# First norm's weights issued by ScalarE, second weight unit split by two engines, gates' columns in parts

## The chip, the cores and the metric

The kernel runs on one core of a Trainium2 chip. The metric is the time of one execution on the device in microseconds (us), the median of several runs. One launch computes the whole reference.

## The reference, cut to what matters

Two blocks work on 256 tokens of width 1024. The first has two layers, each a norm, a mixer (a chunkwise mLSTM with a causal convolution beside a sliding window attention) and an MLP. The second block has two more kinds of attention and a layer that gathers experts. The change touches the head of both layers of the first block:

```python
h = rmsnorm(x, norm_mix_g[l])                  # the first norm's weights are norm_mix_g[0]
proj = h @ w_in[l]
mqk, mv, mo, mi, mf, aq, ak, av, ga, gb = jnp.split(proj, offsets, axis=-1)
...
ig = mi + b_igate ; logf = log_sigmoid(mf + b_fgate)     # the gates, 4 heads
b = jnp.cumsum(fc, axis=-1)
dmat = jnp.where(tril, b[..., :, None] - b[..., None, :] + ic[..., None, :], -jnp.inf)
m_comb = jnp.maximum(m_inter, jnp.max(dmat, axis=-1))
w_intra = jnp.exp(dmat - m_comb[..., None])
s = jnp.einsum('bhld,bhsd->bhls', qc, kc) * w_intra
```

## The kernel before, in words

**Weights come in units.** A unit is 128 x 2048 numbers (1 MB). `layer_units` gives their order in a layer: two of the values (mv 0, mv 1), four mqk, mv 2 and mv 3, four queries (aq 0 to 3), the keys ak, the values av, then the rest. SyncE (SP) issues one DMA per unit into one of three raw slots (`unit_dma`, L470); a slot is free when the signal lo_ready has counted its last user. ScalarE (ACT) rounds the unit to w_hi (`split_hi`, L546), VectorE (DVE) makes the rest w_lo = raw - w_hi (`split_lo`, L553), and TensorE (PE) multiplies in three passes (`passes`, L579 to L581). In some places Pool makes the rest instead (`split_lo_by_pool`, L575). All engines run their own program in order and meet by semaphores; there is no planner.

**The start of layer 0.** SP issues the first tile of tokens x (L479), the first norm's weights, one row of 4 KB given to 128 partitions (L483), the first unit in two halves (L507), the second tile of tokens, and then the units. ACT issues the DMA of the small parameters (L1534, `columns`), squares tile 0 (L684, `norm_act`), rounds both halves of unit 0 (L560, `first_hi`), rounds the transposed tokens (L715, `tile_act`), squares tile 1 and rounds unit 1 (`split_hi`). DVE norms tile 0 (L700, `norm_dve`), makes the rests of unit 0 (L566, `first_lo`) and of the tokens (L721, `tile_dve`), then the rest of unit 1, and only then norms tile 1. Pool makes constants, waits for the small parameters to turn one part of them round (L1524), and then makes one over the root of each tile's mean square (L690 and L693, `norm_pool`). PE transposes tile 0 (L708), multiplies tile 0 with units 0 and 1, in the middle of that transposes tile 1, and multiplies tile 1 with both (`by_tile`). Every engine's order is the order of its program.

**The gates, in both layers.** After mqk 3 PE makes the gates' product. ACT and DVE turn it into rows of 4 x 256; the last one on DVE is L1200 (signal gate_m). Behind unit aq 0 PE spreads each head's row over 128 partitions (`gate_columns`, L834): four products of depth 4, which the profile shows as eight instructions, into the banks att 0 and att 1. In the middle of unit aq 1 it turns the other rows into columns (`gate_more_columns`, L841; signal columns_done). Behind aq 1 stand two products of keys and queries (`kq`, L853 and L854), whose first waits for acol_ready: the copy by DVE of these columns to memory (L1218, in `decay`).

The order of ACT around it is: round a later unit, take aq 0 out of its bank when that unit is done (`take`, L1053), four sigmoids of the convolution (L992, behind a table load), round the next unit but one (L546), take aq 1. DVE's order is: the rest of that unit (L553), then `decay`. Pool multiplies the sigmoids into qk (L1481, eight times 128 x 256) from the first sigmoid on.

Of the kernel before, what the change touches and what calls it, by code (L numbers as in the profile page):

```python
# [7 lines left out]
F32 = mybir.dt.float32  # L8
# [3 lines left out]
ALU = mybir.AluOpType  # L12
# [3 lines left out]
P = 128  # L16
D, SEQ, DEPTH = 1024, 256, 2
# [24 lines left out]
UNIT = 2048  # L42
# [19 lines left out]
def ring_places():  # L62
# [17 lines left out]

    "hi_ready": "a unit's rounded part is made", "lo_ready": "and the rest of it: its raw slot is free",
    "first_hi": "the rounded part of half of the first unit", "first_lo": "and the rest of it",
    "first_loaded": "half of the first unit is here", "x_loaded_too": "the second tile of tokens is here",
    "unit_done": "TensorE is through with a unit", "tile_done": "and with its first tile of tokens", "emptied_act": "ScalarE has emptied a product's bank",
    "emptied_dve": "VectorE has emptied a product's bank",
# [178 lines left out]
class Counts:  # L264
# [10 lines left out]
    def mark(self, name, key=0, by=1):  # L275

        assert (name, self.scope, key) not in self.where, (name, key)
        self.total[name] = self.total.get(name, 0) + by
        self.where[name, self.scope, key] = self.total[name]
        return by  # L280
# [17 lines left out]
def build(nc, A, out, known):  # L298
# [5 lines left out]
    with ctx:  # L304
# [158 lines left out]
        def unit_dma(sp, u):  # L463

            g = counts.unit(u)
            src = A["units2"][u * P:(u + 1) * P, :] if counts.scope == "second" else A["units"][counts.scope, u * P:(u + 1) * P, :]
            if LAST_AT_HOME[g] is not None:
                sp.wait_ge(S["lo_ready"], LAST_AT_HOME[g] + 1)
            s = HOME[g]
            sp.dma_start(raw[s], src).then_inc(S[f"w_loaded{s}"], mark(f"w_loaded{s}", u, 16))  # L470

        def sync_program(sp):
            def rows_of(w):
                return w.broadcast_to([P, D])
# [5 lines left out]
                        S["x_loaded" if t == 0 else "x_loaded_too"], 16)  # L480

            tokens(0)
            sp.dma_start(g_next, rows_of(A["norm_mix_g"][0:1, :])).then_inc(S["g_loaded"], mark("g_loaded", "mix", 16))  # L483
            for l in range(DEPTH):
                counts.scope = l
                for u, unit in enumerate(units):
# [69 lines left out]
        def first_hi(act, half):  # L556

            cols = slice(half * UNIT // 2, (half + 1) * UNIT // 2)
            act.wait_ge(S["first_loaded" if half == 0 else f"w_loaded{HOME[0]}"], 16)
            nc.scalar.copy(w_hi[:, SLOT[0], cols], raw[HOME[0]][:, cols]).then_inc(S["first_hi" if half == 0 else "hi_ready"], 1)  # L560

        def first_lo(dve, half):

# [232 lines left out]
        def layer_pe(pe, l):  # L796
            def step(u, first_time=True):

                name, i, kind = units[u]
                if first_time:  # L800
                    if (l, u) == (0, 0):
                        pe.wait_ge(S["first_lo"], 1)
                    else:
                        pe.wait_ge(S["lo_ready"], counts.unit(u) + 1)
                    for p in BEFORE.get((name, i), []):
                        emptied(pe, *p)
                    if name == "wo" and i < 2:
                        pe.wait_ge(S["y_lo"], at("y_lo", 2 * i + 1))
                    if name == "down" and i % 2 == 0:
                        pe.wait_ge(S["ff_lo"], at("ff_lo", i + 1))  # L810
                xh, xl = (xb_hi, xb_lo) if name in ("bm", "wo", "down") else (xa_hi, xa_lo)
                return BANKS[name, i], SLOT[counts.unit(u)], xh, xl
# [15 lines left out]
                               k == 0, k == KT - 1)  # L828
                m.then_inc(S["gate_done"], mark("gate_done"))

            def gate_columns():
                pe.wait_ge(S["gate_m"], at("gate_m"))
                for h in range(M_HEADS):
                    nc.tensor.matmul(att[h // 2][:, (h % 2) * SEQ:(h % 2 + 1) * SEQ], ident[0:M_HEADS, h:h + 1].broadcast_to([M_HEADS, P]), g_M,  # L834
                                     start=True, stop=True)

# [81 lines left out]
            for u, (name, i, kind) in enumerate(units):  # L918
                if (name, i) in (("mv", 1), ("wo", 3), ("up", 1), ("down", 15)):
                    continue  # L920
                if (name, i) == ("mv", 0):
                    by_tile(pe, step, u, (0, 4), (True, False), (False, True), "mv",
                            lambda t: tile_pe(pe, "mix", 1) if t == 0 else None, "mix", l == 0)
                elif (name, i) == ("wo", 2):
                    by_tile(pe, step, u, (0, 4), (True, False), (False, True), "wo", lambda t: tile_pe(pe, "mlp", 0) if t == 1 else None)
                elif (name, i) == ("up", 0):
                    by_tile(pe, step, u, (0, 4), (True, False), (False, True), "up", lambda t: tile_pe(pe, "mlp", 1) if t == 0 else None, "mlp")
                elif (name, i) == ("down", 14):
                    by_tile(pe, step, u, (4, 4), (False, False), (True, True), "down",
                            lambda t: early_tile(l + 1) if t == 1 and l + 1 < DEPTH else None)  # L930
                else:
                    b, s, xh, xl = step(u)
                    j = TURNED_WITHIN.get((name, i))
                    within = {("gb", 3): turn_hm, ("aq", 1): gate_more_columns}.get((name, i), lambda: None)
                    between = within if j is None else (lambda: turn_probs(j))
                    if name in ("ga", "gb") or name == "up" and i >= 4:
                        unit_wide(b, s, xa, ("u", u), between)
                    elif kind == "F":
                        unit_f(b, s, xh, xl, ("u", u), {("bm", 0): "hm", ("ba", 0): "ha"}.get((name, i)), between)
                    elif kind == "V":  # L940
                        unit_v(b, s, xh, xl, ("u", u))
                    elif name == "down":
                        unit_t(b, s, xh, xl, 4 * (i // 2 % 2), i < 2, False, ("u", u))
                    else:
                        unit_t(b, s, xh, xl, 4 * (i % 2), i % 2 == 0, i % 2 == 1, ("u", u), between)
                if (name, i) in TURNED_WITHIN:
                    pv(TURNED_WITHIN[name, i])
                if (name, i) in SCORED_AFTER:
                    scores(SCORED_AFTER[name, i])
                if (name, i) == ("mqk", 3):  # L950
                    gate_products()
                elif (name, i) == ("aq", 0):
                    gate_columns()
                elif (name, i) == ("aq", 1):
                    kq(0)
                    kq(1)
                elif (name, i) == ("aq", 3):
                    num_product(0)
                    kq(2)
                elif (name, i) == ("ak", 0):  # L960
                    num_product(1)
                    kq(3)
                elif (name, i) == ("av", 0):
                    num_product(2)
                elif (name, i) == ("mo", 0):
                    num_product(3)
                elif (name, i) == ("up", 2):
                    turn_up()


        def layer_act(act, l):
# [111 lines left out]
            if l == 0:  # L1083
                norm_act(act, "mix", 0)
                first_hi(act, 0)
                first_hi(act, 1)
                tile_act(act, xa_hi, "mix", 0)
                norm_act(act, "mix", 1)
                split_hi(act, 1)
            else:  # L1090
                split_hi(act, 0)
                norm_act(act, "mix", 0)
                split_hi(act, 1)
                tile_act(act, xa_hi, "mix", 0)
                norm_act(act, "mix", 1)
                split_hi(act, 2)
# [68 lines left out]
        def layer_dve(dve, l):  # L1165
# [222 lines left out]
                    S["emptied_dve"], mark("emptied_dve", ("wo", 2 * half + t)))  # L1388

            if l == 0:  # L1390
                dve.wait_ge(S["g_loaded"], at("g_loaded", "mix", "start"))
                norm_dve(dve, "mix", 0, g_next)
                for half in range(2):
                    first_lo(dve, half)
                    tile_dve(dve, xa_hi, xa_lo, "mix", 0, [half])
                split_lo(dve, 1)
                norm_dve(dve, "mix", 1, g_next)
            else:
                split_lo(dve, 0)
                mlp_add(dve, l - 1, 0, 0)  # L1400
# [69 lines left out]
        def layer_pool(pool, l):  # L1470
            norm_pool(pool, "mix", 0)
            if l > 0:
                split_lo_by_pool(pool, 1)
            norm_pool(pool, "mix", 1)

            nc.gpsimd.memset(mv[:, :, :, M_DV:VW], 1.0).then_inc(S["pads_ready"], mark("pads_ready", 0))
            nc.gpsimd.memset(mqk[:, :, 0:CONV_K - 1], 0.0).then_inc(S["pads_ready"], mark("pads_ready", 1))
# [53 lines left out]

        def start_act(act):
            counts.scope = "start"
            act.dma_start(columns[:], A["columns"]).then_inc(S["params_loaded"], mark("params_loaded", 0, 16))  # L1534

        def start_dve(dve):
# [864 lines left out]
```

## Time and profile before

| what | value |
|---|---|
| median of 3 runs | 1753.12 us (1752.78 to 1753.4) |
| profiled execution, its own time | 1752.94 us |
| its span, first to last instruction | 1751.2 us |
| mean granted clock of TensorE | 0.985 of full speed |
| busy: PE, PE weight loads, DVE, ACT, Pool | 92%, 68%, 66%, 48%, 22% |
| DMA, mean over the span | 265 GB/s; some 420 GB/s in the last third |

Times in rows are microseconds from the start of the span. A bracket behind a row gives the engine's idle time before it and what ended it. The clock of a stretch is given as a share of 2.4 GHz. In the first two thirds of the span PE is busy nearly throughout and the DMA engines are not; in the last third, where experts are gathered, it is the other way round.

### The profile page before, as it was taken

Reading aid. Unit: us, or ns where it says so; the run is one execution under the profiler, and the core shown is the slowest. Engines: PE = TensorE matmul, PEld = TensorE weight load, DVE = VectorE, ACT = ScalarE, POOL = GpSimd, SP = SyncE. Lnnn points to the kernel's source line nnn. Section 1 sums busy time; section 2 is a strip of 40 time slices with the busy share of each in tenths; the row PEclk is TensorE's granted clock in tenths of the full one; section 3 lists DMA queues with packets and bytes.
Section 4 is the critical chain, followed back from the end, with each engine's and each line's share of the span. In section 5 each row is a group of like instructions: output and inputs, shape, how many; then the busy total and the mean of one; then the engine's idle time right before and its main releaser. Section 6 shows DMA issues by size and latency. Waiting matters only on the chain.

```text
span 1751.2 us, 21314 instructions
## 1 busy us (share of the span) xinstructions
PE 1613.2 (92%) x8160; PEld 1183.5 (68%) x8160; DVE 1159.2 (66%) x2030; ACT 835.1 (48%) x1555; POOL 379.0 (22%) x374
## 2 busy tenths in 40 slices
PE   7999999999999999999999999799987788778786
PEld 6998998888898899888889998455522232222232
DVE  5757865666665776566675556788676767767654
ACT  4456635333455664533355545454444444444443
POOL 0100001000120000100050102565543444334440
PEclk9999999999999999999999999999999999999999
DMA  7444454555544355455544365999999999999996
GB/s 293 161 144 145 152 209 155 198 185 187 198 166 140 125 183 214 168 193 192 186 151 145 145 217 194 414 421 421 422 421 421 422 421 422 422 421 422 421 421 270
DMA packets 67206, 464.43 MB, mean 265 GB/s; under 512 B 7457, under 2 KB 9633, under 8 KB 11809
## 3 DMA queue, kind: packets, MB, share of 16 engines
q0 software_dynamic: 36864, 268.45, 36.9%
q1 hardware_dynamic: 29952, 194.29, 30.8%
q8 instruction: 64, 1.05, 0.2%
q10 hardware_dynamic: 288, 0.33, 0.1%
q14 instruction: 38, 0.30, 0.0%
HBM read 462.00 MB, written 1.05 MB: 264 GB/s over the span
## 4 chain that ended last, share of the span: by engine, by line
PE 65%; DMA 21%; DVE 6%; issue 4%; ACT 3%; POOL 0%; SPq 0%; POOLq 0%; ACTq 0%
PE acc L579 13%; PE acc L581 13%; PE acc L580 13%; DMA arena<-in_peer_uv,arena 10%; DMA row_w_lo<-in_peer_uv,arena 5%; PE att L604 5%; DMA row_w_hi<-in_peer_uv,arena 4%; PE acc L1718 4%; PE acc L1721 4%; PE acc L604 3%; PE att L605 3%; PE acc L605 1%; DVE w_lo L553 1%; DVE arena L2132 1%; PE att L904 1%
## 5 line engine op out<-in xcount | busy, mean ns | idle before, releaser
L553 DVE TENSOR_TENSOR w_lo<-arena,w_hi 128x2048 fp32r<-128x2048 f32 x171 | 391.7, 2300 | 172.8 <-ACT w_hi L546 172.5
L546 ACT CAST w_hi<-arena 128x2048 fp32r<-128x2048 f32 x175 | 333.6, 1907 | 121.8 <-PE acc L581 100.2
L1840 ACT ACTIVATE arena<-arena 128x1 f32<-128x1 f32 x256 | 51.9, 203 | 322.7 <-DVE arena L2132 139.5
L2132 DVE SCALAR_TENSOR_TENSOR arena<-arena 128x1024 f32<-128x1024 f32 x114 | 139.3, 1223 | 84.9 <-DMA arena<-in_peer_uv,arena 83.1
L579 PE MATMUL acc<-xa,w_hi 128*128 128x256 f32 x672 | 192.9, 287 | 0.0
L580 PE MATMUL acc<-xa,w_lo 128*128 128x256 f32 x672 | 190.8, 284 | 0.0
L581 PE MATMUL acc<-xa,w_hi 128*128 128x256 f32 x672 | 190.7, 284 | 0.0
L1718 PE MATMUL acc<-arena,gate_raw 128*128 128x512 f32 x226 | 128.1, 650 | 46.8 <-ACT gate_raw L1850 46.3
L2326 POOL DMA_INDIRECT arena<-in_peer_uv,arena x114 | 129.6, 1137 | 151.4 <-PE acc L1721 141.1
L604 PE MATMUL att<-xa,w_hi 128*128 128x512 f32 x384 | 136.0, 398 | 0.0
L579 PEld LDWEIGHTS acc<-xa,w_hi 128*128 128x128 f32 x672 | 129.2, 192 | 3.6 <-issue 3.0
L580 PEld LDWEIGHTS acc<-xa,w_lo 128*128 128x128 f32 x672 | 129.2, 192 | 0.2
L581 PEld LDWEIGHTS acc<-xa,w_hi 128*128 128x128 f32 x672 | 129.2, 192 | 0.0
L579 PE MATMUL acc<-w_hi,xb 128*128 128x512 f32 x320 | 125.2, 391 | 0.0
L581 PE MATMUL acc<-w_lo,xb 128*128 128x512 f32 x320 | 124.7, 390 | 0.0
L580 PE MATMUL acc<-w_hi,xb 128*128 128x512 f32 x320 | 124.6, 389 | 0.0
L1721 PE MATMUL acc<-arena,gate_raw 128*128 128x512 f32 x226 | 120.8, 617 | 0.0
L579 PE MATMUL acc<-xb,w_hi 128*128 128x256 f32 (+1 forms) x336 | 114.1, 340 | 0.4 <-DVE xb L721 0.4
L1850 ACT ACTIVATE gate_raw<-ident,arena 128x128 f32<-128x128 f32 x255 | 102.4, 401 | 23.4
L1718 PEld LDWEIGHTS acc<-arena,gate_raw 128*128 128x128 f32 x226 | 37.5, 197 | 112.1 <-ACT gate_raw L1850 96.3
L690 POOL TENSOR_TENSOR small<-small 128x1 f32<-128x1 f32 x11 | 2.7, 245 | 494.9 <-ACT arena L684 494.9
L605 PE MATMUL att<-xa,w_lo 128*128 128x256 f32 x384 | 107.8, 281 | 0.0
(309 smaller groups left out, 3545.7 us busy)
## 6 DMA issues: line engine op xcount, KB each, us to landing
arena<-in_units SPq DMA_DIRECT2D x175, 1024.0 KB, 4.8
arena<-in_bias SPq DMA_DIRECT2D x1, 2048.0 KB, 9.3
arena<-in_peer_uv,arena POOLq DMA_INDIRECT x114
x_res<-in_x SPq DMA_DIRECT2D x2, 512.0 KB, 6.5
arena<-in_norm_mix_g SPq DMA_DIRECT2D x2, 512.0 KB, 6.9
arena<-in_units SPq DMA_DIRECT2D x2, 512.0 KB, 8.1
arena<-in_norm_mlp_g SPq DMA_DIRECT2D x2, 512.0 KB, 6.6
arena<-in_norm_g SPq DMA_DIRECT2D x2, 512.0 KB, 5.8
```

Of the source, the lines that this page charges most:

```text
L546: nc.scalar.copy(w_hi[:, s, :], raw[HOME[g]]).then_inc(S["hi_ready"], 1)
L553: nc.vector.tensor_tensor(w_lo[:, s, :], raw[HOME[g]], w_hi[:, s, :].bitcast(F32), ALU.subtract).then_inc(S["lo_ready"], 1)
L579: nc.tensor.matmul(out_, lh, rh, start=first, stop=False)
L580: nc.tensor.matmul(out_, ll, rh, start=False, stop=False)
L581: return nc.tensor.matmul(out_, lh, rl, start=False, stop=last)
L604: nc.tensor.matmul(banks[n_], h[:, k, col_], x2[:, :, k, :], start=k == 0, stop=False)
L605: m = nc.tensor.matmul(banks[n_][:, 0:SEQ], lw[:, k, col_], x2[:, 0, k, :], start=False, stop=k == 7)
L1718: m = nc.tensor.matmul(row_sums[t][0][:], diag[n % 4], rows_ring[PLACE[n]][:, D:D + 512], start=first, stop=last)
L1721: nc.tensor.matmul(row_sums[t][1][:], diag[n % 4], rows_ring[PLACE[n]][:, D + 512:ROW], start=first, stop=last).then_inc(S["rows_multiplie ...
L1850: nc.scalar.activation(diag[n % 4], ident[:], ACT.Copy, scale=d).then_inc(S["diag_ready"], 1)
L2132: nc.vector.scalar_tensor_tensor(row, row, 1.0, hn[:, n // SLOTS, :], ALU.mult, ALU.mult, accum_out=dots[:, n:n + 1]).then_inc(S["rows_use ...
L2326: nc.gpsimd.indirect_dma_start(rows_ring[PLACE[n]], None, A["peer_uv"], bass.IndirectOffsetOnAxis(ap=expert[:, n:n + 1], axis=0)).then_inc ...
```

## The change

Three edits. The DMA of the first norm's weights goes from SP's queue to ACT's, as the first thing that ACT does, under a signal of its own. In layer 0 the second unit is rounded by ACT in two halves, DVE makes the rest of the first half and Pool that of the second, and DVE norms tile 1 ahead of that instead of behind. In both layers two of the four heads' gate rows are spread in the middle of unit aq 0, and the other two behind it.

```diff
@@ sync_program
             tokens(0)
-            sp.dma_start(g_next, rows_of(A["norm_mix_g"][0:1, :])).then_inc(S["g_loaded"], mark("g_loaded", "mix", 16))
@@ unit_dma
+            if LAST_AT_HOME[g] == 1:
+                sp.wait_ge(S["first_lo"], 2)
@@ new functions
+        def second_hi(act, half):
+            cols = slice(half * UNIT // 2, (half + 1) * UNIT // 2)
+            if half == 0:
+                act.wait_ge(S[f"w_loaded{HOME[1]}"], at(f"w_loaded{HOME[1]}", 1))
+            nc.scalar.copy(w_hi[:, SLOT[1], cols], raw[HOME[1]][:, cols]).then_inc(S["first_hi" if half == 0 else "hi_ready"], 1)
+
+        def second_lo(eng, op, half):
+            cols = slice(half * UNIT // 2, (half + 1) * UNIT // 2)
+            if half == 0:
+                eng.wait_ge(S["first_hi"], 2)
+            else:
+                eng.wait_ge(S["hi_ready"], 2)
+                eng.wait_ge(S["lo_ready"], 1)
+            op(w_lo[:, SLOT[1], cols], raw[HOME[1]][:, cols], w_hi[:, SLOT[1], cols].bitcast(F32), ALU.subtract).then_inc(
+                S["first_lo" if half == 0 else "lo_ready"], 1)
@@ layer_pe, step
                         pe.wait_ge(S["first_lo"], 1)
+                    elif (l, u) == (0, 1):
+                        pe.wait_ge(S["first_lo"], 2)
+                        pe.wait_ge(S["lo_ready"], 2)
@@ layer_pe, gate_columns
-            def gate_columns():
+            def gate_columns(heads):
                 pe.wait_ge(S["gate_m"], at("gate_m"))
-                for h in range(M_HEADS):
+                for h in heads:
@@ layer_pe, units
-                    within = {("gb", 3): turn_hm, ("aq", 1): gate_more_columns}.get((name, i), lambda: None)
+                    within = {("gb", 3): turn_hm, ("aq", 0): lambda: gate_columns((0, 1)), ("aq", 1): gate_more_columns}.get((name, i), lambda: None)
...
                 elif (name, i) == ("aq", 0):
-                    gate_columns()
+                    gate_columns((2, 3))
@@ layer_act, l == 0
                 norm_act(act, "mix", 1)
-                split_hi(act, 1)
+                second_hi(act, 0)
+                second_hi(act, 1)
@@ layer_dve, l == 0
-                dve.wait_ge(S["g_loaded"], at("g_loaded", "mix", "start"))
+                dve.wait_ge(S["g_first_loaded"], 16)
...
-                split_lo(dve, 1)
                 norm_dve(dve, "mix", 1, g_next)
+                second_lo(dve, nc.vector.tensor_tensor, 0)
@@ layer_pool
             norm_pool(pool, "mix", 1)
+            if l == 0:
+                second_lo(pool, nc.gpsimd.tensor_tensor, 1)
@@ start_act
+            act.dma_start(g_next, A["norm_mix_g"][0:1, :].broadcast_to([P, D])).then_inc(S["g_first_loaded"], 16)
             act.dma_start(columns[:], A["columns"]).then_inc(S["params_loaded"], mark("params_loaded", 0, 16))
```

## Rows read from the trace of the kernel before

**Rows 1.** The page, part 1: busy time, share of the span, instructions of each engine.
```profile
PE 1613.2 (92%) x8160; PEld 1183.5 (68%) x8160; DVE 1159.2 (66%) x2030; ACT 835.1 (48%) x1555; POOL 379.0 (22%) x374
```

**Rows 2.** The chain that ended last, first 20 us: start us, us, what.
```profile
3.27 11.14 DMA arena<-in_units
14.43 1.91 ACT w_hi L546
16.36 2.30 DVE w_lo L553
```

**Rows 3.** Timeline of the first 8 us: SP's and ACT's issues, Pool, DVE.
```profile
0.80 0.40 ACTq L1534 DMA_DIRECT2D columns<-in_columns  x1
1.23 0.42 SPq L483 DMA_DIRECT2D arena<-in_norm_mix_g  x1
...
4.83 0.31 POOL L1524 TENSOR_SCALAR columns<-columns 128x32 f32<-128x32 f32 x1 [3.04 <-DMA columns<-in_columns]
...
7.46 1.41 DVE L700 SCALAR_TENSOR_TENSOR arena<-x_res,small,arena 128x512 f32<-128x512 f32 x2 [7.46 <-DMA arena<-in_norm_mix_g]
```

**Rows 4.** Windows: stretch, us, busy of the engines, clock, DMA share, GB/s.
```profile
5.00:6.00 1.00, 0.00 (x0) 0.00 (x0) 0.00 (x0) 0.71 (x2) 0.32 (x2) 1.00 0.91 229
...
13.00:14.00 1.00, 0.93 (x2) 0.83 (x3) 1.00 (x2) 0.74 (x2) 0.18 (x1) 1.00 1.03 434
```

**Rows 5.** Timeline of 10 to 21 us: all engines around unit 1.
```profile
10.67 1.04 ACT L560 CAST w_hi<-arena 128x1024 fp32r<-128x1024 f32 x1 [0.20 <-DMA arena<-in_units]
...
14.19 0.56 POOL L693 TENSOR_TENSOR small<-small,minus_half 128x1 f32<-128x1 f32 x1
...
17.91 0.63 PE L581 MATMUL acc<-w_lo,xa 128*128 128x512 f32 x1
18.57 1.41 DVE L700 SCALAR_TENSOR_TENSOR arena<-x_res,small,arena 128x512 f32<-128x512 f32 x2
...
18.71 0.49 PE L579 MATMUL acc<-w_hi,xa 128*128 128x512 f32 x1 [0.17 <-DVE w_lo L553]
...
20.89 1.03 PE L708 MATMUL att<-ident,arena 128*128 128x128 f32 x8
```

**Rows 6.** Pool by source line: ns min/median/max; L575 all, L1481 at 73 to 77 and 77 to 80.2.
```profile
L575 POOL TENSOR_TENSOR w_lo<-arena,w_hi x4: 4595/4596/5057, 267.8 to 1076.5; 128x2048 fp32r<-128x2048 f32 x4
...
L1481 POOL TENSOR_TENSOR arena<-arena x5: 632/727/737, 73.8 to 76.4; 128x256 f32<-128x256 f32 x5
...
L1481 POOL TENSOR_TENSOR arena<-arena x3: 732/737/2684, 76.4 to 77.8; 128x256 f32<-128x256 f32 x3
```

**Rows 7.** Timeline of PE at aq 0 and aq 1, both layers, and one window of layer 0.
```profile
71.10 1.99 PE L834 MATMUL att<-arena,ident 4*128 4x256 f32 x8
73.02 0.41 PE L579 MATMUL acc<-xa,w_hi 128*128 128x256 f32 x1
...
77.59 1.05 PE L841 MATMUL att<-ident,arena 4*128 4x4 f32 x8
...
508.18 0.39 PE L579 MATMUL acc<-xa,w_hi 128*128 128x256 f32 x1
...
511.25 1.05 PE L841 MATMUL att<-ident,arena 4*128 4x4 f32 x8
...
74.00:75.00 1.00, 1.00 (x7) 1.00 (x6) 0.00 (x0) 1.00 (x3) 1.00 (x2) 0.50 0.83 319
```

**Rows 8.** Timeline: gate_m on DVE, then aq 0 taken and the first kq, both layers.
```profile
66.70 0.41 DVE L1200 SCALAR_TENSOR_TENSOR arena<-arena 4x256 f32<-4x256 f32 x1
...
71.21 0.60 ACT L1053 ACTIVATE arena<-acc 128x512 f32<-128x512 f32 x1 [1.15 <-PE acc L581]
...
81.53 0.59 PE L853 MATMUL att<-arena 128*128 128x256 f32 x2
...
506.37 0.60 ACT L1053 ACTIVATE arena<-acc 128x512 f32<-128x512 f32 x1 [1.15 <-PE acc L581]
...
515.40 0.30 PEld L853 LDWEIGHTS att<-arena 128*128 128x128 f32 x2 [0.24 <-DVE small L1218]
```

More of the change, by code:

```diff
@@ L82 @@
     "first_hi": "the rounded part of half of the first unit", "first_lo": "and the rest of it",
+    "g_first_loaded": "the first norm's weights are here",
     "first_loaded": "half of the first unit is here", "x_loaded_too": "the second tile of tokens is here",
```

## The prediction

> **What bounds the kernel now.** I read the page first: PE is busy 92% of the span and no other engine comes near it [rows 1]. So an edit counts where PE is late or waits, and in the first two layers a microsecond that PE loses or gains is handed on to the end: ACT, DVE and the weight DMAs there wait for PE's signals. The three edits lie at two kinds of place, and I read each from the view that shows who comes last there.
>
> At the start I took the chain of waits. Its first 20 us are the DMA of unit 1, landed at 14.43, ACT's rounding, DVE's rest, and then PE at 18.71 [rows 2, 5]. PE comes off unit 0 just before: its last product of that starts at 17.91, and it then shows 0.17 us of idle [rows 5]. The start is balanced: PE is not waiting long, and whoever makes unit 1 ready later than 18.7 makes the kernel longer.
>
> At the gates I took the timeline of PE. The eight small products hold PE from 71.10 to 73.02, and behind them PE's granted clock is 0.50, that is 1.2 GHz instead of 2.4, though PE had no gap ahead of that [rows 7]. The cost can be read by laying the layers side by side, as layer 1 keeps its clock: from the first product of aq 1 to the block in its middle it is 77.59 - 73.02 = 4.57 us in layer 0 and 511.25 - 508.18 = 3.07 in layer 1, so the low clock costs 1.50 us [rows 7].
>
> What comes behind that matters as much. The first kq waits for DVE's copy of the columns. In layer 1 PE's weight load stands idle 0.24 us for it [rows 8]: there the side chain, aq 0 taken by ACT, sigmoids, rounding, DVE's rest, copy, already comes last. It runs from 506.37 to 515.40, 9.03 us [rows 8]. In layer 0 the same distance is 81.53 - 71.21 = 10.32 us with no wait of PE, as PE is the slow one there [rows 8].
>
> **Edit 1, the DMA on ACT's queue.** SP loses one issue of 0.42 us [rows 3], and x's second tile, units 0 and 1 are issued that much earlier. The bytes stay the same and the 16 DMA engines are at a share of 0.91 and 1.03 in the stretches around the transfers [rows 4], so they gain from 0 to 0.45 us. I take 0.2: unit 1 lands at 14.2, since the engines are nearer to full than to empty. ACT issues one DMA more (0.40 us, [rows 3]), while it has nothing but its table load to do before the tokens arrive: nothing. The small parameters are now queued behind the 512 KB of norm weights. Pool waits for them at 4.83 ahead of the root that tile 0's norm needs, and the norm weights landed at 7.46 [rows 3]; if both land at 7.5, Pool is through (0.31 and under 1 us, [rows 3, 5]) at 8.8, and DVE's norm starts 1.3 us later than 7.46. What hides it is ACT, which takes the transposed tile only behind its second half of unit 0, whose rounding ends at 11.7 [rows 5]. I count nothing; beyond some 1.5 us of delay it would show one for one. If the tokens land later, since they now share the engines with the norm weights, the same cover holds.
>
> **Edit 2, unit 1 in halves.** Before, PE starts on it 18.71 - 14.43 = 4.28 us behind the landing [rows 2, 5]. Now ACT rounds two halves of 1.04 us [rows 5], so both are there 2.1 us behind the landing, at 16.3. Pool takes 4.596 us for a whole unit [rows 6], 2.3 for half: twice DVE's 2.30 per unit [rows 2]. Alone, Pool is done at 16.3 + 2.3 = 18.6, PE starts at 18.7, and the split has bought nothing. DVE's norm of tile 1 starts when the root is there, 14.19 + 0.56 = 14.75 [rows 5], ends at 16.2, and DVE's half (1.2 us) follows until 17.4.
>
> The unknown is how Pool and DVE get on. At 77 to 80 us, while DVE makes a rest, one of Pool's products of 0.73 takes 2.68 us, with the shape of five others at 0.63 to 0.74 [rows 6]. The extra 1.95 us is nearly a whole rest of DVE (2.30, [rows 2]), so I read it as one waiting for the other. DVE's half starts at 16.2 and Pool's wants to at 16.3, so one goes after the other: 16.2 + 1.2 + 2.3 = 19.7, or 19.5 when unit 0 and with it the square of tile 1 come 0.2 earlier. PE starts unit 1 at 19.5 in place of 18.7: **+0.8 us**. The bounds are -0.4 (no hindrance, DMA gain in full) and +1.0. The other order, Pool first, gives the same sum. The Trainium skill, SBUF — State Buffer, section "SBUF: two separate sides", says that a VectorE instruction with two SBUF inputs and a GpSimd instruction that reads SBUF take the shared port pair as "an exclusive lock, not a bandwidth split". By that rule it is the sum above; were it a split in which each slows by a quarter, it would be 19.2, and +0.5.
>
> The norm of tile 1, moved ahead, was not late: it ran at 18.57 for 1.41 us, to 19.98, and PE came to the transposes at 20.89 [rows 5]. Nothing gained. SP's wait for unit 4's slot has a condition more, and it is met before Pool's half is: nothing.
>
> **Edit 3, the rows in two places.** gate_m is made by 66.70 + 0.41 = 67.1 [rows 8], and the middle of aq 0 is some 3 us ahead of 71.0, at 68.1: PE doesn't wait, with 1 us to spare. The weak stretch is cut in half, to 0.96 us, as long as the other block, L841 with 1.05, behind which the clock stood [rows 7]. So the clock stays up in layer 0, and PE reaches kq 1.50 earlier, at 80.0.
>
> But aq 0 is now done half a block later: 0.96 us, with the way in and out 1.1. ACT's take, the sigmoids, the rounding, DVE's rest and the copy all stand behind that. Layer 0: 71.21 + 1.1 + 9.03 = 81.3; PE waits there 1.3 us and starts at 81.3 in place of 81.53: **-0.2**. Layer 1 had no low clock to win back and was already waiting: **+1.1**, bounds +0.9 and +1.2.
>
> **Sum:** 0.8 - 0.2 + 1.1 = +1.7 us. On the profiled execution 1752.94 gives 1754.6; its own time is 0.18 below the median, and against the median 1753.12 I get 1754.8. Its own range is 1753.8 to 1755.4. About 0.2%, 3.5 us, is what a measurement of this kernel can tell from no change, so this is within it.
>
> **Rivals.** (a) Slower: the waits that the change makes (some 1.4 us ahead of unit 1, 1.3 ahead of kq in either layer) let the clock down or keep it down. Each time costs 1.50 [rows 7]: 1756.3 for one, 1757.8 for two. It decides from the point where a wait is followed by products at 0.50. For it: the clock did fall behind weak work; against: each wait has full work before and behind it. The Trainium skill, TensorE: Matmul & The Clock Gate, part 1 on the clock gate, has the low clock as the default that activity releases and idleness brings back; by that the fall at 73, without idleness, is not explained, and the new waits are the danger.
> (b) Pool and DVE don't hinder each other: the start costs 0 to -0.4 in place of +0.8, and the sum is +0.5 to +0.9, 1753.8. Against it is the product of 2.68 us.
> (c) Faster: the side chain isn't what holds kq, the 1.50 comes in full, layer 1 stays, the start gives 0.4: 1751.2. Against it is the wait of 0.24 us.
> (d) The third edit doesn't do what it says: the clock falls in layer 0 all the same. PE is then at kq at 81.6, and the sum is +2.0: 1755.1.
>
> **Numbers.** The forecast has a chance of 0.50, (a) 0.17, (b) 0.15, (c) 0.07, (d) 0.08; 0.03 is for the unforeseen. The range runs from 1752.9, under (b), to 1756.7, over (a) with one fall. Over 1756.6 needs two falls or more: 0.07. Faster by over 0.2% would be under 1749.6, which no case reaches: 0.02. The rest, 0.91, is no change.
>
> **What would show it.** Right: Pool's half starts when DVE's ends, PE's first product of unit 1 at 19.2 to 19.8; no window of 0.50 behind 71; PE idle ahead of kq 1.0 to 1.5 us in both layers, released by DVE L1218; aq 0 taken 1.1 us later against gate_m in both. Wrong: Pool and DVE side by side with the durations of [rows 6]; PE on unit 1 before 18.5; a kq without a wait; a window of half clock in layer 0 or 1 outside the first 19 us.

## The result, and the profile after

The changed kernel takes 1758.19 us (median of 9 runs, 1756.3 to 1758.76), the kernel before 1752.78 in its 9 runs of the same series (1751.36 to 1754.05). The ratio is 1.0027, with a 95% interval from 1.0017 to 1.0037: slower, by 5.4 us in the medians and by 4.7 by the ratio, where 1.7 were forecast and 1756.7 us was the upper end of the range. The profiled execution took 1758.48 us, its span 1756.7.

The page after, part 1, against [rows 1]: the work is the same, and what grew is the time in which PE does nothing.

```profile
span 1756.7 us, 21318 instructions
...
PE 1611.7 (92%) x8160; PEld 1181.7 (67%) x8160; DVE 1160.2 (66%) x2030; ACT 835.2 (48%) x1556; POOL 381.3 (22%) x375
```

I put the k-th product of PE after beside the k-th before. PE starts tile 1 on unit 0 at 26.51 us, where it was 22.89: 3.6 us are lost in the first 27. At the gates of layer 1 the shift rises from 3.7 to 4.97 us, it is 5.18 at 993 us, and it ends at 5.5.

**The start after**, timeline of the first 21 us, against [rows 3] and [rows 5]:

```profile
0.80 0.41 ACTq L1560 DMA_DIRECT2D arena<-in_norm_mix_g  x1
1.24 0.45 ACTq L1561 DMA_DIRECT2D columns<-in_columns  x1
...
6.40 1.06 ACT L704 ACTIVATE arena<-x_res 128x1024 f32<-128x1024 f32 x1 [3.40 <-DMA x_res<-in_x]
...
9.42 0.31 POOL L1550 TENSOR_SCALAR columns<-columns 128x32 f32<-128x32 f32 x1 [7.63 <-DMA columns<-in_columns]
...
10.66 1.41 DVE L720 SCALAR_TENSOR_TENSOR arena<-x_res,small,arena 128x512 f32<-128x512 f32 x2 [10.66 <-POOL small L713]
...
14.02 1.06 ACT L704 ACTIVATE arena<-x_res 128x1024 f32<-128x1024 f32 x1
...
14.14 0.76 PE L599 MATMUL acc<-w_hi,xa 128*128 128x512 f32 x1 [0.64 <-DVE xa L741]
...
15.07 1.98 ACT L569 CAST w_hi<-arena 128x1024 fp32r<-128x1024 f32 x2
...
16.11 1.41 DVE L720 SCALAR_TENSOR_TENSOR arena<-x_res,small,arena 128x512 f32<-128x512 f32 x2 [0.38 <-POOL small L713]
...
17.13 2.61 POOL L579 TENSOR_TENSOR w_lo<-arena,w_hi 128x1024 fp32r<-128x1024 f32 x1 [1.06 <-ACT w_hi L569]
...
17.44 3.39 DVE L579 TENSOR_TENSOR w_lo<-arena,w_hi 128x1024 fp32r<-128x1024 f32 x1
...
20.89 0.80 PE L599 MATMUL acc<-w_hi,xa 128*128 128x512 f32 x1 [2.36 <-DVE w_lo L579]
```

Read it from below. PE begins unit 1 at 20.89 in place of 18.71, released by DVE's half. That took 3.39 us, started while Pool's was running. Pool's began at 17.13, released by ACT's rounding of unit 1, and DVE's at 17.44, behind the norm of tile 1, which ran from 16.11. Both stand behind one thing: ACT squared tile 1 only from 14.02, where it was 12.58 before. PE's own first product is at 14.14 in place of 13.07, for the same reason that ACT was late: the norm of tile 0 began at 10.66 in place of 7.46. Pool held that, waiting until 9.42 for the small parameters. The chain of waits says it in two lines:

```profile
1.24 8.10 DMA columns<-in_columns
...
17.52 3.32 DVE w_lo L579
```

**The clock behind that wait**, windows of the kernel after (stretch, us, busy of PE, PEld, DVE, ACT and Pool, granted clock, DMA share, GB/s):

```profile
17.00:20.00 3.00, 1.53 (x7) 0.92 (x5) 3.00 (x2) 0.06 (x1) 2.72 (x3) 1.00 0.94 386
20.00:21.00 1.00, 0.11 (x1) 0.12 (x1) 0.83 (x1) 0.00 (x0) 0.00 (x0) 0.80 0.06 22
21.00:22.00 1.00, 1.00 (x3) 0.81 (x4) 0.00 (x0) 0.00 (x0) 0.00 (x0) 0.50 0.44 57
```

The clock falls while PE stands, and the first products of unit 1 run at 1.2 GHz. From the start of unit 1 to the start of tile 1 PE needs 26.51 - 20.89 = 5.62 us, where it was 22.89 - 18.71 = 4.18: 1.44 us more.

**The gates after**, timeline of PE, its weight loads and ACT in both layers, against [rows 7] and [rows 8]:

```profile
71.83 1.12 PE L857 MATMUL att<-arena,ident 4*128 4x256 f32 x4
...
76.06 0.60 ACT L1076 ACTIVATE arena<-acc 128x512 f32<-128x512 f32 x1 [2.40 <-PE acc L601]
...
85.12 0.30 PEld L876 LDWEIGHTS att<-arena 128*128 128x128 f32 x2 [1.14 <-DVE small L1242]
...
511.31 0.60 ACT L1076 ACTIVATE arena<-acc 128x512 f32<-128x512 f32 x1 [2.40 <-PE acc L601]
...
520.37 0.30 PEld L876 LDWEIGHTS att<-arena 128*128 128x128 f32 x2 [1.14 <-DVE small L1242]
```

```profile
77.00:81.00 4.00, 4.00 (x33) 3.86 (x32) 0.00 (x0) 3.99 (x6) 2.32 (x4) 1.00 0.72 256
```

In layer 0 the clock stays at 1.00 behind the smaller blocks, and PE hands the gain over to a wait for DVE's copy. In layer 1 it only waits longer, 1.14 us in place of 0.24. The chain from aq 0 taken to kq is 85.12 - 76.06 = 9.06 us in one and 520.37 - 511.31 = 9.06 in the other; it was 9.03.

### The profile page after: what moved, and what is told of

Same layout as the page of the kernel before. It is cut to its first block, busy times and chain, and to the rows that moved or that the text cites. A ratio compares the mean times of both kernels' runs of the same rounds, so it can differ in the third digit from the quotient of the medians.

```text
span 1756.7 us, 21318 instructions
## 1 busy us (share of the span) xinstructions
PE 1611.7 (92%) x8160; PEld 1181.7 (67%) x8160; DVE 1160.2 (66%) x2030; ACT 835.2 (48%) x1556; POOL 381.3 (22%) x375
## 4 chain that ended last, share of the span: by engine, by line
PE 60%; DMA 23%; DVE 7%; issue 5%; ACT 3%; POOL 1%; SPq 0%; ACTq 0%; POOLq 0%; DVEq 0%
PE acc L599 12%; PE acc L601 12%; PE acc L600 12%; DMA arena<-in_peer_uv,arena 12%; DMA row_w_lo<-in_peer_uv,arena 5%; PE att L624 5%; PE acc L1745 3%; PE acc L624 3%; DMA row_xa<-in_peer_uv,arena 3%; PE acc L1748 3%; PE att L625 3%; DMA row_w_hi<-in_peer_uv,arena 2%; PE acc L625 1%; DVE w_lo L555 1%; ACT w_hi L548 1%
```

## The experiments

Each kernel was timed in 5 rounds beside the kernel before on the same chip. The medians of before in the four series were 1752.95, 1752.87, 1753.28 and 1753.52 us, and each median below stands against that of its own series. The intervals are some 0.09% to either side, 1.6 us, so that parts under a microsecond are read from the traces.

**The third edit alone**, on the kernel before:

```diff
-            def gate_columns():
+            def gate_columns(heads):
...
+  within = {..., ("aq", 0): lambda: gate_columns((0, 1)), ...}
...
-                    gate_columns()
+                    gate_columns((2, 3))
```

> The kernel before with the third edit alone. Theory (the side chain behind aq 0 sets kq): layer 0 changes by -0.3 to +0.1 us at kq, as the clock stays up and PE then waits 0.9 to 1.4 us for the copy of DVE; layer 1 loses 1.2 us at kq. In all +0.9 to +1.4 us. Rival (the loss of the changed kernel behind the start comes from its shifted clock, not from this edit): no wait at kq in layer 0, PE there 1.5 us earlier, in all -1.5 to 0 us.

Measured: 1754.75 against 1752.95 us, +1.8, ratio 1.0007 (0.9998 to 1.0015). Its weight loads:

```profile
81.51 0.30 PEld L853 LDWEIGHTS att<-arena 128*128 128x128 f32 x2 [1.14 <-DVE small L1218]
...
516.68 0.30 PEld L853 LDWEIGHTS att<-arena 128*128 128x128 f32 x2 [1.14 <-DVE small L1218]
```

kq is where it was in layer 0 (81.53 before), and 1.28 us later in layer 1. Each layer has the wait. The rival, in which layer 0 gains its 1.5 us, falls. The median is 0.4 above the theory's upper end; by the ratio it is +1.2, inside it, and the interval holds 1. In the profile the shift against the kernel before is 1.28 us at this kq and 1.49 at 993 us, but 3.0 at the end: the stage that gathers experts put on another 1.5.

**The first two edits alone**, the changed kernel with the rows back in one block.

```diff
-            def gate_columns(heads):
+            def gate_columns():
...
-                    gate_columns((2, 3))
+                    gate_columns()
```

> The changed kernel with the gate rows put back in one block behind aq 0: the first two edits alone. Theory: PE begins with tile 1 3.6 us later than before, as in the changed kernel; at the gates of layer 1 nothing is lost. If the clock falls behind the block in layer 0 as before, +3.6 us in all; if it doesn't, because the block lies elsewhere against the clock's steps, +2.4. Rival (the start's delay is partly taken in later): under +2 us in all.

Measured: 1756.11 against 1752.95, +3.2, ratio 1.0017 (1.0009 to 1.0026). With the +1.8 above the two make 5.0 of the 5.4. In its profile unit 1 begins where it did in the changed kernel, but with another wait and another clock:

```profile
20.88 0.50 PE L599 MATMUL acc<-w_hi,xa 128*128 128x512 f32 x1 [1.73 <-DVE w_lo L579]
```

```profile
21.00:22.00 1.00, 1.00 (x5) 0.82 (x6) 0.00 (x0) 0.00 (x0) 0.00 (x0) 1.00 0.50 66
```

The expected 3.6 us was missed: here the clock stayed up, and all products up to the end of the layers are 2.1 to 2.3 us late. The program up to there is that of the changed kernel, so the fall is not in every execution. The two waits are not equal either. In both profiles the products of unit 0 first come 0.43 us apart and then 0.23; here that changed at 18.5 us, in the changed kernel at 17.2, so that PE left unit 0 later and stood 1.73 us in place of 2.36. That profiled execution (1755.13 us) was the fastest of the twelve.

**The first edit alone**, on the kernel before:

```diff
-            sp.dma_start(g_next, ...norm_mix_g...)
...
+            act.dma_start(g_next, ...norm_mix_g...)
             act.dma_start(columns[:], A["columns"])
```

> The kernel before with the first edit alone: the norm weights' DMA on ACT's queue ahead of the small parameters. Theory (Pool waits for the small parameters, which now land at 9.4 us in place of 4.8, and holds the norm of tile 0): PE's first product at 14.1 in place of 13.07, unit 1 begun at 19.3 to 19.5 in place of 18.7, in all +0.6 us with the clock kept and up to +2 with a fall. Rival (the edit is free, the halves alone cost): PE's first product at 12.7, in all -0.3 to 0.

Measured: 1753.87 against 1752.95, +0.9, ratio 1.0004 (0.9995 to 1.0012).

```profile
9.42 0.31 POOL L1524 TENSOR_SCALAR columns<-columns 128x32 f32<-128x32 f32 x1 [7.62 <-DMA columns<-in_columns]
...
14.13 0.77 PE L579 MATMUL acc<-w_hi,xa 128*128 128x512 f32 x1 [0.64 <-DVE xa L721]
...
19.33 0.50 PE L579 MATMUL acc<-w_hi,xa 128*128 128x512 f32 x1 [0.73 <-DVE w_lo L553]
```

The delay is all there with the first edit alone: 1.06 us on PE's first product and 0.62 on unit 1. The rival that the edit is free falls in the trace; the median alone would not have told, as the intervals of this run and of the next hold 1.

**The second edit alone**, on the kernel before.

```diff
-                split_hi(act, 1)
+                second_hi(act, 0)
+                second_hi(act, 1)
...
-                split_lo(dve, 1)
                 norm_dve(dve, "mix", 1, g_next)
+                second_lo(dve, nc.vector.tensor_tensor, 0)
...
+                second_lo(pool, nc.gpsimd.tensor_tensor, 1)
```

> The kernel before with the second edit alone: unit 1 rounded in halves, one rest by DVE and one by Pool, tile 1's norm ahead. Theory (one waits for the other): the two rests run one after the other, together 3.5 us, and PE begins unit 1 at 19.7 to 20.0 in place of 18.7: +1.0 to +1.3 us, and up to 1.5 more if the clock falls in the wait. Rival (they run side by side, and in the changed kernel it was the late start alone): PE at 18.8, +0.1 us.

Measured: 1753.53 against 1752.95, +0.6, ratio 1.0002 (0.9993 to 1.0010).

```profile
16.06 1.22 DVE L580 TENSOR_TENSOR w_lo<-arena,w_hi 128x1024 fp32r<-128x1024 f32 x1
...
16.43 3.06 POOL L580 TENSOR_TENSOR w_lo<-arena,w_hi 128x1024 fp32r<-128x1024 f32 x1 [1.73 <-ACT w_hi L570]
...
19.59 0.47 PE L600 MATMUL acc<-w_hi,xa 128*128 128x512 f32 x1 [1.75 <-issue]
```

Now DVE came first and kept its 1.22 us; Pool, begun 0.37 later, took 3.06. PE is at unit 1 at 19.59, +0.88. It is 0.1 us better than the lower end of the theory and far from the rival's 18.8.

**The two issues of ACT swapped** in the changed kernel:

```diff
-            act.dma_start(g_next, ...)
             act.dma_start(columns[:], A["columns"])
+            act.dma_start(g_next, ...)
```

> The changed kernel with ACT's two issues swapped: the small parameters first, the norm weights behind them. Theory (the small parameters' place in the queue made the start late): they are here at 5 us, the norm of tile 0 starts by 8.6, PE's first product at 12.6 to 12.9 in place of 14.14, unit 1 begun at 19.3 to 19.6 in place of 20.88. Against the changed kernel -1.4 us, and -1.4 more where the clock no longer falls in the wait; against the kernel before +1.5 to +2.5. Rival (the norm weights' own transfer beside the tokens is what is late, whatever stands behind it): PE's first product stays at 13.8 or later.

Measured: 1755.29 against 1752.87, +2.4, ratio 1.0015 (1.0006 to 1.0024).

```profile
4.87 0.31 POOL L1550 TENSOR_SCALAR columns<-columns 128x32 f32<-128x32 f32 x1 [3.08 <-DMA columns<-in_columns]
...
8.77 1.41 DVE L720 SCALAR_TENSOR_TENSOR arena<-x_res,small,arena 128x512 f32<-128x512 f32 x2 [8.77 <-DMA arena<-in_norm_mix_g]
...
12.24 0.77 PE L599 MATMUL acc<-w_hi,xa 128*128 128x512 f32 x1 [0.64 <-DVE xa L741]
...
19.00 0.79 PE L599 MATMUL acc<-w_hi,xa 128*128 128x512 f32 x1 [2.23 <-DVE w_lo L579]
```

The place in the queue was it: PE's first product is at 12.24, 1.9 us earlier than in the changed kernel and 0.8 earlier than before the change. The tokens landed at 4.60, as before the change. The halves still keep PE off unit 1 until 19.00, and behind this wait of 2.23 us the clock fell again: from unit 1 to tile 1 PE needs 24.72 - 19.00 = 5.72 us, where it was 4.18.

**Both rests by DVE** in the changed kernel:

```diff
                 second_lo(dve, nc.vector.tensor_tensor, 0)
+                second_lo(dve, nc.vector.tensor_tensor, 1)
...
-                second_lo(pool, nc.gpsimd.tensor_tensor, 1)
```

> The changed kernel with both rests of unit 1 made by DVE, Pool's left out. Theory (the two engines wait for each other): two rests of 1.22 us behind the norm of tile 1, done at 19.9 in place of 20.83, PE on unit 1 0.9 us earlier. Rival (they work side by side, DVE's 3.39 us is a slower DVE alone): DVE's halves together take 3.4 or more, and nothing is gained.

Measured: 1756.27 against 1752.87, +3.4, ratio 1.0020 (1.0011 to 1.0029).

```profile
17.23 2.35 DVE L579 TENSOR_TENSOR w_lo<-arena,w_hi 128x1024 fp32r<-128x1024 f32 x2
...
19.68 0.47 PE L599 MATMUL acc<-w_hi,xa 128*128 128x512 f32 x1 [0.94 <-issue]
```

One engine makes both halves in 2.35 us, from 17.23 to 19.58; the two together needed from 17.13 to 20.83. The rival falls. PE is at unit 1 1.2 us earlier, of which 0.2 were there at its first product already (13.93 against 14.14).

**Products in PE's wait** in the changed kernel. Eight more products run, and nothing reads them.

```diff
                 for n_, u in enumerate((ua, ua + 1)):
+                    if in_halves and t == 0 and n_ == 1:
+                        for _ in range(8):
+                            nc.tensor.matmul(att[3][:], xa_hi[:, 0, 0:P], whi(SLOT[0], "T")[:, 0, :], start=True, stop=True)
```

> The changed kernel with eight products of 128x512 put into the bank att 3 while PE waits for unit 1; their result is used by nothing. Theory (the clock falls because PE is idle there): unit 1 begins at 20.9 as in the changed kernel, but no window behind it is at 0.50, and tile 1 begins 1.4 us earlier; of the times at 1758.2 to 1758.8 of the changed kernel few or none are left, the median near 1756.7. Rival (the fall has another cause): windows at 0.50 behind 20.5 as before, median at 1758.

Measured: 1757.33 against 1752.87, +4.5, ratio 1.0026 (1.0015 to 1.0038), 7 runs from 1756.87 to 1758.34.

```profile
20.87 0.50 PE L599 MATMUL acc<-w_hi,xa 128*128 128x512 f32 x1 [0.19 <-DVE w_lo L579]
...
25.05 0.51 PE L599 MATMUL acc<-w_hi,xa 128*128 128x512 f32 x1 [0.27 <-DVE xa L744]
```

```profile
21.00:22.00 1.00, 1.00 (x5) 0.82 (x6) 0.00 (x0) 0.00 (x0) 0.00 (x0) 1.00 0.47 66
```

In the trace the theory holds: the clock stays at 1.00 and tile 1 starts 1.46 us earlier. But the first two edits' profile kept its clock without filling, so one profile does not prove that the filling did it. PE's last product of unit 0 starts at 18.48 here, between the 18.14 of the changed kernel and the 18.75 of that profile. And the time does not follow as expected: kq of layer 1 is at 518.88, 1.49 earlier than in the changed kernel, while the spans are 1756.5 and 1756.7. Put beside the changed kernel product by product, PE is 1.45 to 1.5 us ahead all through the layers (to 993 us), some 2.0 ahead up to 1270 us, and 0.3 ahead from 1398 us to the end. The gain went in between, in a stretch of the gather stage in which the DMA engines are full. The windows view of the kernel after has there (columns as above):

```profile
1300.00:1400.00 100.00, 80.64 (x164) 29.42 (x162) 69.94 (x183) 42.03 (x130) 44.97 (x41) 0.97 1.01 422
```

With the DMA share at 1.01, at 422 GB/s, what PE wins ahead of this stretch need not reach the end; that this is how it was lost is read from the place alone, no run tested it. So the two groups in the changed kernel's times (four at 1756.3 to 1757.0, five at 1758.2 to 1758.8) can't be put down to the fall at 20 us.

**The copy ahead of the rest**, on the kernel with the third edit alone:

```diff
+                if (name, i) == ("aq", 1):
+                    columns_copy()          # the copy, taken out of decay()
                 if 0 < u < NU - 2 and ...:
                     split_lo(dve, u + 2)
```

> The kernel before with the third edit, and DVE's copy of the columns put ahead of the rest of the later unit. Theory (the side chain behind aq 0, whose last links are that rest and the copy, sets kq): PE has no wait at kq; in layer 0 kq at 80.2 to 80.5 in place of 81.5, in layer 1 0 to 0.2 us earlier than in the kernel before. Against the kernel before -1.0 to -1.4 us where that one's clock falls behind the block, 0 where it doesn't; against the third edit alone -2.2 to -2.6. Rival (Pool's products hold kq, or the unit behind is late): a wait of 0.5 us or more stays ahead of or behind kq.

Measured: 1752.43 against 1752.87, -0.4, ratio 0.9998 (0.9989 to 1.0007).

```profile
77.42 0.17 DVE L1218 COPY small<-att 128x16 f32<-128x16 f32 x1 [5.17 <-PE att L841]
...
80.28 0.59 PE L853 MATMUL att<-arena 128*128 128x256 f32 x2
...
514.17 0.59 PE L853 MATMUL att<-arena 128*128 128x256 f32 x2
```

No wait is left at kq. It comes at 80.28 and 514.17 where the third edit alone had 81.51 and 516.68, and the median goes from 1.8 us above the kernel before to 0.4 below it. The side chain, and in it the copy's place behind DVE's rest, is what held kq.

**The early copy alone**, the block whole; the diff is the one above without the third edit.

> The kernel before with the early copy alone, the gates' rows in one block. Tells apart what the split of the block is worth once the copy no longer holds kq. Theory: layer 1 gains the 0.24 us of the wait at kq; layer 0 gains nothing where its clock falls behind the block. In all -0.1 to -0.3 us; the early copy with the split block was at -0.4. Rival (the copy alone brought that gain): as much as with the split block, or more.

Measured: 1752.11 against 1753.28, -1.2, ratio 0.9993 (0.9984 to 1.0002). The rival fits better here, at least as much as with the split block, but the intervals of the two runs overlap over most of their length. In its profile the clock did not fall behind the whole block:

```profile
70.98 1.99 PE L834 MATMUL att<-arena,ident 4*128 4x256 f32 x8
75.96 1.05 PE L841 MATMUL att<-ident,arena 4*128 4x4 f32 x8
```

That is 4.98 us from block to block, where [rows 7] has 77.59 - 71.10 = 6.49. So the fall that the third edit was to avoid is itself not in every execution. Nor is it bound to layer 0. The time from the start of the whole block (the eight products) to the block in aq 1, in all profiles that have it:

| profile | layer 0, us | layer 1, us |
|---|---|---|
| before | 6.49 | 4.99 |
| first two edits | 6.31 | 4.98 |
| first edit | 4.98 | 6.41 |
| second edit | 6.47 | 4.99 |
| early copy alone | 4.98 | 4.99 |
| first edit in the better order (below) | 4.99 | 6.15 |
| all together, block whole (below) | 6.50 | 4.99 |

Where it is above 6 the granted clock was 0.50 behind the block. In the seven profiles with the split block it fell there in neither layer. How much of the -1.2 is the copy, and how much a clock that happened to stay up, the times do not tell.

**The first edit in the better order**, on the kernel before: the norm weights on ACT's queue, behind the small parameters.

> The kernel before with the norm weights' DMA on ACT's queue behind the small parameters, all else as before. Theory: PE's first product at 12.2 as in the changed kernel with that order, unit 1 landed by 13.2, rounded by 15.1, its rest by DVE by 17.5, PE on it at 17.5 in place of 18.7: -1.2 us at the start, -1.2 to -0.7 in all. Rival (PE is then bound by its own slow products of unit 0 or the clock stays low a step longer): -0.3 to +0.5.

Measured: 1751.80 against 1753.28, -1.5, ratio 0.9992 (0.9983 to 1.0001).

```profile
12.07 0.77 PE L579 MATMUL acc<-w_hi,xa 128*128 128x512 f32 x1 [0.64 <-DVE xa L721]
...
17.61 0.50 PE L579 MATMUL acc<-w_hi,xa 128*128 128x512 f32 x1 [0.70 <-DVE w_lo L553]
```

Unit 1 begins 1.1 us earlier than before, close to the theory's 1.2. The interval just holds 1, so the gain is shown at its place in the trace and not by the times.

**Together**: this order, unit 1 whole and by DVE, and the early copy, once with the block split and once whole.

> The order of the two issues mended, unit 1 whole and by DVE as before, the gates' rows in two places, the copy early. Theory (the parts add up): -1.2 at the start and -1.2 at the gates of layer 0 in the profile, 1750.4 to 1751.5 us. Rival (the gather stage or the clock takes it back): 1752 or more.

> The best version so far with the gates' rows in one block again: issues in the mended order, unit 1 whole and by DVE, the copy early. Tells what the split block is worth. If the block lets the clock down in one of the layers in most executions, 1.3 to 1.5 us more than with the split block in those, median 0.5 to 1.5 above it (ratio to the kernel before 0.999 to 1.000). If the split block's gain is taken by its own additional ways in and out and by luck with the clock, the same within 0.3 us (ratio 0.9988).

Measured: 1751.54 with the block split (ratio 0.9988, 0.9979 to 0.9997) and 1751.76 with the block whole (0.9989, 0.9980 to 0.9998), against 1753.28 and 1753.52. Both are faster than the kernel before by some 1.7 us, with intervals that end below 1, and than the changed kernel by some 7, one series laid against another. The first is at the edge of its theory (1750.4 to 1751.5). The times show no gain of the split, as the second case had it. The profiles do, for kq of layer 0 with the block split and with it whole:

```profile
79.27 0.59 PE L853 MATMUL att<-arena 128*128 128x256 f32 x2
```

```profile
80.85 0.59 PE L853 MATMUL att<-arena 128*128 128x256 f32 x2
```

Of these 1.58 us 0.45 were there from the start; the clock fell behind the whole block in layer 0, and the profile with the split ends 1.2 us earlier. Two medians whose intervals are 1.6 us to either side can't rule out a gain of that size.

## Why the prediction was wrong

The direction of the sum was right, and so was what holds each layer's gates, the side chain. The step that failed is "I count nothing" at the first edit, and with it the size of the second; beside it the sum had nothing for the clock, which the prediction kept as a rival. The two spans differ by 5.5 us where 1.7 were summed. Of the 3.8 between them the start has 1.4 (2.18 in place of 0.8), the clock 1.4, the gates 0.4, and 0.6 is open.

**Edit 1.** The cost was looked for in the right place, Pool's wait for the small parameters, and sized too low. I took them as landed at 7.5 us, when the norm weights had landed before; they came at 9.4. The norm of tile 0 began 3.2 us late in place of 1.3, beyond the 1.5 that ACT's order was said to cover. It covered 2.1: alone the edit puts 1.06 us on PE's first product and 0.62 on unit 1. I had fixed the landing by one transfer's time in its old queue, though two queues now shared the engines and the tokens themselves landed at 6.40 in place of 4.57. The Trainium skill, DMA: Bandwidth & Descriptors, section "Issuing engines are not separate DMA queues", has transfers of all issuing engines interleave on the same 16 engines; the trace agrees, with 1.8 us more for the tokens. That holds where both transfers are issued at the same moment, 0.80; with the norm weights issued at 1.24 the tokens landed at 4.60. The gain on SP's side was sized too low as well: in the better order unit 1 landed at 13.33 in place of 14.43, 1.1 us earlier where 0.2 were taken.

**Edit 2.** +0.8 was forecast and the edit alone gives +0.88, with one engine waiting for the other as foreseen: rival (b) fell. Together with edit 1 it gives 20.89 - 18.71 = 2.18 us. The parts measured singly make 0.62 + 0.88 = 1.5; the other 0.7 is what the two together add. I had tile 1's norm start at 14.75 and the first of the two halves at 16.2. The norm started at 16.11 and the first half, Pool's, at 17.13, since ACT could square tile 1 and round unit 1 only behind the late tile 0. In the run of the second edit alone the first half began at 16.06; from it to the end of the other the two took 3.43 us there and 3.70 here. I had reckoned each edit at the other's old times.

**The clock.** Rival (a) came true in the profile, at the first of its three places: PE's wait ahead of unit 1 was 2.36 us in place of 1.4, the clock fell, and that cost 1.44 us against a price of 1.50. It had a chance of 0.17. Other profiles show that this was in part luck: behind PE's wait ahead of unit 1 the clock also fell with the two issues swapped (2.23 us), and not in the runs of the first two edits (1.73), of the second edit (1.75) and of both rests by DVE (0.94). At kq it did not fall in any profile with that wait.

**Edit 3.** Layer 1 was to lose 1.1, at most 1.2, and lost 1.3 (3.7 to 4.97): the half block with its ways in and out puts some 1.2 us on aq 0, not 1.1. Layer 0 was to gain 0.2 and gained nothing (85.12 against 81.53 + 3.62 = 85.15). The mechanism, the side chain of 9.03 us, stands, shown by the early copy. Rivals (c) and (d) fell. That layer 0 had a low clock to win back and layer 1 none was read from one profile; two of the others with the whole block have it the other way round.

**The sum by these terms** is 2.18 + 1.44 + 0 + 1.3 = 4.9 of the 5.5 that the two spans differ by. The last 0.6 gathers in small steps, 0.2 of it up to 993 us and the rest behind that; I have not found its cause. What the run with products in PE's wait showed of the gather stage also means that the shift at the end need not be the sum of the shifts ahead of it: edit 3 alone has 1.49 us ahead of that stage and 3.0 behind it, and why is open. Its median (+1.8) lies 0.5 above what the trace shows at the gates, its ratio (+1.2) does not, so the times give no reason to look for more there.

## What to carry to other kernels

A transfer that is moved to another queue delays what stands behind it there, however small: follow the last small one to whoever waits for it, and put that ahead of the big one. When two edits act on the same few microseconds, run the second one's arithmetic on the times that the first one leaves. Cutting a block to spare the clock only pays where PE comes last behind it; here the side chain did, and moving one copy of 0.17 us ahead of DVE's rest took away the wait of 1.14 us in both layers. A fall of the clock that one profile shows is one draw: look at several before it becomes a term of a sum.

## What the runs showed of the hardware

- 65 KB on ACT's queue behind a transfer of 512 KB took 8.1 us from issue to landing, and first in the queue 3.9 us.
- 512 KB of tokens, issued by SP at 0.79 us, landed at 6.40 when ACT issued 512 KB at 0.80, and at 4.60 when ACT issued the small parameters at 0.79 and the 512 KB at 1.24.
- Half a unit's rest takes DVE 1.22 us alone, and 3.39 when it begins 0.31 us behind Pool's of the same shape; Pool's takes 2.61 when it begins first and 3.06 when it begins 0.37 us behind DVE's. Whoever comes second ends within 0.15 us of where it would if it had started when the first was done (with 1.22 for DVE and half of Pool's 4.6 us per unit, an estimate). The time in which it is held shows as part of the instruction, not as idle time.
- Behind eight products of depth 4 in one block (1.99 us), with no gap in PE's work, the granted clock fell to 0.50 in one of the two layers in six of seven profiles (layer 0 in four, layer 1 in two) and in neither in the seventh. Behind four such products (1.12 us) it did not fall in seven profiles.
- Behind PE's wait ahead of unit 1 the clock fell with 2.36 and 2.23 us, and not with 1.73, 1.75 and 0.94. The same program up to there gave the 2.36 and the 1.73.
- All but two of the 115 times of the kernel before lie between 1751.4 and 1755.6 us, so a single profile decides about places, and not about a microsecond in the end.
